# A fused two-block forward pass: last two expert units by tile, norm and loads beside them, a query half later, both turns ahead of a first panel

## The reference

```python
def rmsnorm(x, w):
    return x * lax.rsqrt(jnp.mean(x * x, axis=-1, keepdims=True) + 1e-6) * w

# experts: 128 x 128 of them, 16 chosen for each of 8 heads
act = gelu(einsum('phkd,pd->phk', u_table[expert], x))
x = x + einsum('phk,phkd->pd', gate * act, v_table[expert])
x = rmsnorm(x, norm_final_w)                       # the final norm
h = layer_norm(DN_ALPHA * x + 0.5 * (silu(x @ w1) * (x @ w3)) @ w2)   # first feed-forward layer
...
q = h @ w_q                                        # sparse attention: query, scores, softmax, mix
```

## Time and profile before

| what | value |
|---|---|
| median of 3 runs | 2352.18 us (2349.55 to 2353.56) |
| the profiled execution | 2350.93 us |
| its span, first to last instruction | 2348.8 us |
| mean granted TensorE clock | 0.986 of full |
| TensorE busy | 2245.6 us, 96% of the span |
| VectorE, ScalarE busy | 1607.9 us (68%), 1177.1 us (50%) |
| DMA | 390.18 MB, mean 166 GB/s |

### The profile page before, as it was taken

One profiled execution on the slowest core, in us unless ns is written; L12 is line 12 of the kernel. 1 busy time (PEld: TensorE's weight loads), 2 busy tenths in 40 slices (PEclk: granted clock), 3 DMA queues, 4 the chain that ended last, 5 costly groups with the idle time before them and its releaser, 6 DMA issues. The chain is left out here.

```text
span 2348.8 us, 36404 instructions
## 1 busy us (share of the span) xinstructions
PE 2245.6 (96%) x14300; PEld 2005.0 (85%) x14300; DVE 1607.9 (68%) x2800; ACT 1177.1 (50%) x2052; POOL 57.1 (2%) x28
## 2 busy tenths in 40 slices
PE   8988999999999999999998999999999999979998
PEld 8877788999999998888877888988888788868887
DVE  7867546999889985666666556666657555776555
ACT  5522444455554445555555445445443544575444
POOL 0131000111000000000000000000000000000000
PEclk9989999999999999999999999999999999999999
DMA  6462324355444445555536546536555655404552
GB/s 266 144 72 96 137 97 163 117 188 179 147 150 146 145 148 178 195 192 193 196 127 242 197 179 235 198 126 217 188 193 181 245 185 191 148 1 162 197 184 102
DMA packets 78306, 390.18 MB, mean 166 GB/s; under 512 B 9771, under 2 KB 12715, under 8 KB 49740
## 3 DMA queue, kind: packets, MB, share of 16 engines
q1 hardware_dynamic: 76684, 383.59, 45.7%
q0 software_dynamic: 1040, 4.19, 1.6%
q10 hardware_dynamic: 432, 0.33, 0.0%
HBM read 382.83 MB, written 5.24 MB: 165 GB/s over the span
## 5 line engine op out<-in xcount | busy, mean ns | idle before, releaser
L251 DVE TENSOR_TENSOR split_slots<-ring,split_slots 128x1024 fp32r<-128x1024 f32 x404 | 482.2, 1239 | 137.2 <-ACT split_slots L242 137.0
L2873 PE MATMUL banks<-x_transposed,split_slots 128*128 128x512 f32 x1360 | 481.1, 397 | 2.0 <-PEq L454 2.0
L402 DVE SCALAR_TENSOR_TENSOR expert_lo<-ring,expert_hi 128x512 fp32r<-128x512 f32 x512 | 363.5, 715 | 173.8 <-ACT expert_hi L397 172.9
L242 ACT ACTIVATE split_slots<-ring 128x1024 fp32r<-128x1024 f32 x404 | 403.0, 1050 | 155.5 <-PE banks L393 139.4
L397 ACT ACTIVATE expert_hi<-ring 128x512 fp32r<-128x512 f32 x512 | 323.2, 632 | 267.2 <-PE banks L393 267.2
L2874 PE MATMUL banks<-x_transposed,split_slots 128*128 128x256 f32 x1360 | 382.0, 281 | 0.0
L2873 PEld LDWEIGHTS banks<-x_transposed,split_slots 128*128 128x128 f32 x1360 | 256.0, 188 | 63.7 <-issue 2.2
L391 PE MATMUL banks<-x_transposed,expert_hi 128*128 128x256 f32 x1024 | 296.9, 290 | 5.5 <-DVE expert_lo L402 5.5
L392 PE MATMUL banks<-x_transposed,expert_hi 128*128 128x256 f32 x1024 | 290.7, 284 | 0.0
L393 PE MATMUL banks<-x_transposed,expert_lo 128*128 128x256 f32 x1024 | 290.6, 284 | 0.0
L2874 PEld LDWEIGHTS banks<-x_transposed,split_slots 128*128 128x128 f32 x1360 | 257.6, 189 | 1.5
(11 more groups left out here) (484 smaller groups left out, 4154.6 us busy)
## 6 DMA issues: line engine op xcount, KB each, us to landing
ring<-in_ffn_w SPq DMA_DIRECT2D x132, 1024.0 KB, 4.8
ring<-in_peer_u SPq DMA_DIRECT2D x128, 512.0 KB, 3.3
ring<-in_peer_v SPq DMA_DIRECT2D x128, 512.0 KB, 3.4
ring<-in_w_in SPq DMA_DIRECT2D x16, 1024.0 KB, 5.4
ring<-in_sgu_w_in SPq DMA_DIRECT2D x16, 1024.0 KB, 4.9
ring<-in_peer_wq SPq DMA_DIRECT2D x8, 1024.0 KB, 5.7
ring<-in_sgu_w_out SPq DMA_DIRECT2D x8, 1024.0 KB, 4.8
ring<-in_kv_w SPq DMA_DIRECT2D x6, 1024.0 KB, 4.8
```

What stands on the lines that cost most here:

```text
L242: act.activation(self.parts[:, b, 0, p], self.k.w.slot(g)[:, p], ACT.Copy).then_inc(self.high_done, 1)
L251: ins = dve.tensor_tensor(self.parts[:, b, 1, p], self.k.w.slot(g)[:, p], self.parts[:, b, 0, p].bitcast(F32), ALU.subtract)
L402: return dve.scalar_tensor_tensor(dst, src, scale, hi.bitcast(F32), ALU.mult, ALU.subtract)
L2873: pe.matmul(out(j, slice(0, 2 * SEQ)), lh, k.xT.both[:, c, :, :], start=(c == 0), stop=False)
```

## The change

1. `peer`: the last two v units are multiplied tile by tile (tile 0 of both units, then tile 1), and each tile signals `v_done`. The additions wait for their own tile. The gain row and the first feed-forward panel are loaded near the end of the expert stage, into places that the memory plan keeps for them (`next_splits`, `next_gain`), and the panel is split there: its high parts on ScalarE, its low halves on VectorE, one ahead of each addition. Tile 0's square, sum and root are taken there too. The root's table is loaded in the middle of the v units. TensorE gets 8, 8 and 3 stand-ins.
2. `final_norm`: only tile 1's square and root are left, then both tiles' scaling. TensorE turns tile 0 and does four stand-ins; tile 1 is turned in `high_first` of the feed-forward layer.
3. `high_first`, x on the right: both turns stand ahead of the first 16 products.
4. `query_and_attend`: the second half of query panel 3 moves from step 3 to step 4, after its scores.

```diff
 class Beginning:
-    def __init__(self, k):
+    def __init__(self, k, parts=None):
+        self.k, self.g, self.parts = k, k.w.taken, parts
...
 def high_first(...)
         before.turn(pe, near)
+        before.turn(pe, far)
         if x_on_right:
             banks()
-        else:
-            before.turn(pe, far)
         pe.wait_ge(before.highed[0], 3)
         for j in range(2) if x_on_right else (1,):
             high(j, near)
-        if x_on_right:
-            before.turn(pe, far)
         pe.wait_ge(before.highed[0], 4)
...
 def pick_and_run_experts(k, room)
+        begin = Beginning(k, room.next_splits)
@@ block.sync
+            sp.wait_ge(w_low, KEYS)
+            sp.dma_start(room.final_gain[:, :], k.a["norm_final_w"].partition_broadcast(P)).then_inc(gain_landed, 16)
+            sp.wait_ge(tiles.low_done, 2 * (2 * KEYS - 2))
+            k.w.issue(sp, begin.g + 1)
+            sp.wait_ge(tiles.low_done, 2 * 2 * KEYS)
+            k.w.issue(sp, begin.g + RING)
+            sp.wait_ge(gain_landed, 16)
@@ block.tensor
-            for m in range(KEYS):
+            for m in range(KEYS - 2):
                 v_products(m)
+            for i in range(TILES):
+                for m in (KEYS - 2, KEYS - 1):
+                    pe.wait_ge(w_low, m + 1)
+                    for half in range(2):
+                        pe.wait_ge(tiles.low_done, 2 * (KEYS + m) + half + 1)
+                        ins = v_tile(m, half, i)
+                ins.then_inc(v_done, 1)
+            stand_in(pe, k, 8, 7)
+            pe.wait_ge(added, 1)
+            stand_in(pe, k, 8, 7)
+            pe.wait_ge(squared, 1)
+            stand_in(pe, k, 3, 7)
@@ block.scalar
+                if m == KEYS // 2:
+                    act.activation(k.final_stat[:, 3, 0:1], k.eps[:, 0:1], ACT.Sqrt)
+            act.wait_ge(w_low, KEYS)
+            begin.highs(act)
+            act.wait_ge(added, 1)
+            act.activation(acts[...], k.x[:, 0, :], ACT.Square, accum_out=k.final_stat[:, 0, 0:1]).then_inc(squared, 1)
+            act.wait_ge(squared, 1)
+            act.activation(k.final_stat[:, 1, 0:1], k.final_stat[:, 0, 0:1], ACT.Sqrt, bias=k.eps[:, 0:1], scale=1.0 / D)
@@ block.vector
-            dve.wait_ge(tiles.eaten, 4 * KEYS)
             for t in range(TILES):
+                begin.low(dve, t)
+                dve.wait_ge(v_done, t + 1)
                 dve.tensor_tensor(k.x[:, t, :], accumulated(k, t), k.x[:, t, :], ALU.add).then_inc(added, 1)
...
 def final_norm(k)
@@ block.sync
-            sp.dma_start(gain[:, :], k.a["norm_final_w"].partition_broadcast(P)).then_inc(landed, 16)
             k.stream(sp)
@@ block.tensor
-            for i in range(TILES):
-                turn_chunks(pe, k, k.x[:, i, :], i, banks, 4, normed)
+            turn_chunks(pe, k, k.x[:, 0, :], 0, banks, 4, normed)
+            stand_in(pe, k, 4, 7)
@@ block.scalar
-            for i in range(TILES):
-                act.activation(sq[:, i, :], k.x[:, i, :], ACT.Square, accum_out=stat[:, 0, i:i + 1]).then_inc(squares, 1)
-            act.wait_ge(squares, TILES)
-            act.activation(stat[:, 1, :], stat[:, 0, :], ACT.Sqrt, ...).then_inc(rooted, 1)
-            begin.highs(act)
+            act.activation(sq[:, :], k.x[:, 1, :], ACT.Square, accum_out=stat[:, 0, 1:2]).then_inc(squared, 1)
+            act.wait_ge(squared, 1)
+            act.activation(stat[:, 1, 1:2], stat[:, 0, 1:2], ACT.Sqrt, ...).then_inc(rooted, 1)
             highs(act)
@@ block.vector
             for i in range(TILES):
+                if i == 1:
+                    dve.wait_ge(rooted, 1)
+                dve.reciprocal(stat[:, 2, i:i + 1], stat[:, 1, i:i + 1]).then_inc(recip, 1)
+                dve.wait_ge(recip, i + 1)
...
-            begin.lows(dve)
             lows(dve)
-        k.before = Before((written, 4), (high, 4), (written, 4), ((written, 1),))
+        k.before = Before((high, 4), (high, 4), (written, 4), turn=turn_last)
...
 def query_and_attend(...)
                 if n < 2:
                     queries(pe, n + 1)
+                if n == 4:
+                    queries(pe, 3, (1,))
...
-                if n == 3:
-                    queries(pe, 3, (1,))
```

More of the change, by code:

```diff
@@ L442, in lasting_splits @@
     @contextmanager
-    def lasting_splits(self):
+    def lasting_splits(self, written=None):
         with ExitStack() as ctx:
             self.split_parts = self.sb(ctx, "split_slots", [P, BUFFERS, 2, SLOT], F32R)
+            if written is not None:
+                self.split_parts = written
             yield
@@ L1984, in __init__ @@
             self.picks = PickRoom(k, early)
+        with ExitStack() as late:
+            self.next_splits = k.sb(late, "split_slots", [P, BUFFERS, 2, SLOT], F32R)
+            k.sb(late, "norm_gain_bias", [P, 2, D])
+            self.final_gain = k.sb(late, "final_gain", [P, D])
+        k.next_splits, k.next_gain = self.next_splits, self.final_gain
         self.acts = k.sb(ctx, "expert_weights", [P, KEYS, SEQ])
@@ L2103, in pick_and_run_experts @@
         assert PICKS_AT > FIRST_SCATTER + 2
+        begin = Beginning(k, room.next_splits)
+        gain_landed, squared = (k.sig.new() for _ in range(2))
         (landed, numbered, q_copied, scored, score_copied, found, hits, chosen, reduced, vs, expd, turned, copied,
@@ L2176, in scatter, with v_tile @@
                 ins.then_inc(made, 1)
+            def v_tile(m, half, i):
+                hi, lo = tiles.halves(KEYS + m, half)
+                own = slice(i * P, (i + 1) * P)
+                return passes(pe, k.psum[:, 2 * i + half, :], (weighted[:, m % 4, 0, own], weighted[:, m % 4, 1, own]),
+                              (hi, lo), m == 0, m == KEYS - 1)
             def v_products(m):
@@ L2184, in v_products @@
                     pe.wait_ge(tiles.low_done, 2 * n + half + 1)
-                    hi, lo = tiles.halves(n, half)
                     for i in range(TILES):
-                        own = slice(i * P, (i + 1) * P)
-                        ins = passes(pe, k.psum[:, 2 * i + half, :], (weighted[:, m % 4, 0, own], weighted[:, m % 4, 1, own]),
-                                     (hi, lo), m == 0, m == KEYS - 1)
+                        ins = v_tile(m, half, i)
                     ins.then_inc(tiles.eaten, 1)
```

36 lines of the change are left out of this document (19 added, 17 removed).

## The result

The changed kernel takes 2331.45 us (median of 4 runs, 2330.84 to 2332.13) where the kernel before takes 2351.61 in the same comparison. The ratio is 0.9912, with a 95% interval of 0.9896 to 0.9929. The profiled execution took 2332.13 us (span 2330.0, mean granted clock 0.987), 18.8 us less than that of before.

The account below looks back on a forecast made before the run. TensorE, busy 96% of the span, was taken as the bound, so only closing its gaps counts. Gains of 3.4 + 3.8 + 4.4 = 11.6 us from the median 2352.18 gave 2340.5 us, range 2337.0 to 2345.0.

Parts of the forecast that it names:

- 3.4 + 3.8 + 4.4 = 11.6 us: Whole kernel: gains of the expert tail with final norm, both turns ahead, and the query half, added up.
- part 1: Expert tail and final norm: early panel load and half the norm end the first panel sooner; 3.4 us (1.7 to 6.1).
- part 3: Attention stage: moving the query half shortens ScalarE's wait and avoids the lower clock; 4.4 us (2.8 to 4.6).
- The two costs put at nothing: Expert stage: the last low part has 0.6 us margin; the root's table load delays one split within its margin.
- TensorE's 8 + 8 + 3 stand-ins: Expert tail: at 0.11 us each, 0.22 at the lower clock, they end before the next stage starts at 1237.2.
- 4.8 to 5.8 us after the block's end: Final norm: sign for part 1, when the first product comes, instead of 11.3 us.
- Rival (a): Expert tail: low clock through two panels or a load near 1234.5, part 1 brings nothing; 2344.0 us; chance 0.13.
- part 2: First panels at three places: second turn runs in TensorE's idle time, 1.28 us each; 3.8 us (2.5 to 3.9).
- Rival (c): Attention stage: ScalarE's copy waits for a late half, part 3 gives little; price 4.4 us, 2345.0; chance 0.07.
- (b): Expert tail: load early and full clock, part 1 brings 6.1 us; 2337.9 us; chance 0.15.
- (d): Expert tail: additions wait for a late panel load, slower than before; 2357.5 us for landing at 1248; chance 0.02.
- (e): Whole kernel: the gaps close but a later wait, such as the weight ring, takes them; about 2349 us; chance 0.03.

Follow-up runs that it names:

- experiments 5 and 6: 5: the changed kernel again, 2332.85 us; 6: the changed kernel with its final statistics in reused memory, so no later buffer moves, 2340.13 us; kernel before 2350.64.
- experiment 7: The changed kernel with 4 stand-in calls behind the first addition, instead of 8 and then 3 behind the square: 2333.03 us against 2332.85.
- experiments 12 and 15: 12: changed kernel with additions first and 64 bytes of shift, 2320.57 us; 15: 12 with the last block's buffers another 32 bytes further on, 2317.34 us.
- experiments 3 and 11: 3: kernel before with both turns ahead alone, 2344.91 us; 11: kernel before with expert tail and final norm alone, without the 32 bytes, 2348.98 us.

## Why the prediction was right and wrong

**A term was missing; the sum of what was costed came out near, in part by luck.** The failed step is the sum, "3.4 + 3.8 + 4.4 = 11.6 us": it has no term for the reservation of the final statistics, which the diff shown ahead of the prediction leaves out and which I took for no edit at all. Nothing in it had an instruction, so nothing had a row. What the runs showed in its place is that the 32 bytes change the distance between the operands of products in stages that the change does not touch, and that this was worth 7.3 us in this kernel (experiments 5 and 6; 3.2 alone). The prediction's last sentence asked for other stages that "grow by the same microseconds". Loops and stages shrank instead, most of them, and I had no case for that among the rivals: all of them, on both sides, were about waits.

The three parts together gave 10.5 us against 11.6. That this is so near is luck in part: part 1 came out lower than forecast and part 3 higher. The end, 2340.13 against 2340.5, is nearer still because the kernel before took 2350.64 in that comparison and not 2352.18.

**Part 1: right in its chain, wrong in what ends it, and too high.** The load landing behind VectorE, the four operations at 1.2 us and the additions' end came within 0.3 us of the working (all of it 5 us earlier in the trace, since u was shorter and the clock did not fall in v). The two costs put at nothing, the tighter splits and the root's table, were nothing: v took 348.1 us, as in the profiles with the old tail where the clock did not fall in it. "TensorE's 8 + 8 + 3 stand-ins [...] end before that" failed, and first by count. The 0.11 us of the earlier trace rows are one product's, and a call makes two, so 22 products stood behind the first addition, not 11. They took 4.35 us at a mean clock of 0.61. At the full-clock distance of 0.12 us (16 took 1.95 here) I estimate 2.7 us, which would still have ended 0.4 us after the additions; the clock did the rest. So the next stage began 9.1 us after the last expert product, where the working had 7.2. From there the first product came in 4.4 us (the working had 4.0 to 5.1; its "4.8 to 5.8 us after the block's end" does not follow from its own times, which give 4.3 to 5.4), and the panel ran at the full clock in 5.79 us, as forecast (5.7). That makes 2.3 us of the 3.4.

Alone the part measured -1.8 us with zero in the interval. The 3.4 were counted from one profiled execution whose panel ran at 0.76, and of eight such profiles four ran the panel at the full clock and had 1.7 us less to give. Rival (a), "the new wait eats the first part", has the number of part 1 by itself better than the forecast did, but not its reason: neither did the low clock hold through the panel nor did the load land near 1234.5. With part 2 beside it 0.5 to 2.3 us are left. Gain and panel landed 6.9 us after the first issue (1218.89 to 1225.8), near the 7.1 of before. The estimate of 5.6 us by the Trainium skill ("DMA: Bandwidth & Descriptors", Anatomy of one DMA) was too low; the page fits its line to single DMAs issued from GpSimd, and these are two from SyncE's queue. The row was the better guide.

In experiment 7 TensorE was idle for 4.6 us of the stretch instead of 4.1, and the mean clock was 0.82 instead of 0.91. The Trainium skill ("TensorE: Matmul & The Clock Gate", Why this matters for your kernels) says that idle between bursts of matmuls brings the half rate back, and the trace agrees. That is the section to look in; the prediction named another one of the same page for it.

**Part 2: right.** 4.4 us measured by the medians (1.4 to 7.5 by the interval), 3.8 forecast, and 1.4 to 1.5 at each of the three places in the trace, where 1.28 was the forecast. What the text said of the first feed-forward panel, "already in part 1", hid that the gain there depends on part 2.

**Part 3: right in every link.** The copy's wait went from 4.80 to 1.94 (forecast 1.8), the query copy no longer held TensorE, and the clock did not fall behind it (in experiment 6's profile it fell 12 us later). The size, 4.4 forecast, is 3.9 against the profiled execution and about 5.5 against the six profiles with more low clock; the runs gave 6.1. Rival (c) fell.

**Rivals (b), (d) and (e).** (b) had the full clock ahead of the panel right but gave it to an early load, which did not come: the load took 6.4 us from its issue. (d) did not happen, (e) neither.

## What to carry to other kernels

Read a diff for what it reserves, not only for what it issues: one small buffer between two operands changed the pace of thousands of products, and an unused one of 64 bytes gave as much as a careful rearrangement, by the medians more (13.1 against 10.5 us). When a gain does not match its parts, compare the length of the stages that were not touched, in a stretch where the clock is full, before looking for a wait. And a low-clock stretch in one profile is worth its price only as often as other executions have it too.

## What the runs showed of the hardware

- The pace of back-to-back products depends on the distance between their two operands in the on-chip memory. At full clock (500 to 860 us) the 128x256 products of u that follow each other directly start 119.8 ns apart in the mean at the old distance, 118.5 with 32 bytes more, 115.2 with 64 (115.6 and 115.9 in experiments 12 and 15), 118.5 with 96 and 119.6 with 128. Shifting both operands together by 32 bytes does nothing (119.8). What in the memory causes it was not found; that it is the distance within 128 bytes fits u, and fits the feed-forward stages only in part.
- Not every stage gains from the same shift: 32 bytes made the first and the last feed-forward stage 1.9 us shorter and the other two 0.6 to 1.0 us longer, each of some 162 us. For the second stage that is not shown to be the bytes: it took 163.0 us without any shift in experiments 3 and 11 too, where 162.1 and 163.1 are its values before and after.
- Where the clock falls varies between executions whose instructions are the same up to there. At the panel behind the expert tail (19.7 to 20.0 or 21.4 to 22.2 us) that moves a profile by 1.7 us and more, and in the attention stage (156.3 or 157.2 to 158.4 us) by some 1.6 us.
